# Gate and up products of a feed-forward phase in one 512-column and one 256-column matmul instead of three of 256 columns

## What is computed

```python
def swiglu(h, w_gate, w_up, w_down):
    return (jax.nn.silu(h @ w_gate) * (h @ w_up)) @ w_down
# x = x + 0.5 * swiglu(rmsnorm(x, g), ...)   D_MODEL 1024, D_FF 2816, 256 tokens
```

## Time and profile before

| | us |
|---|---|
| median of 3 runs | 2785.74 (2781.83 to 2786.46) |
| the profiled execution | 2786.89 |
| its span in the trace | 2785.1 |

### The profile page before, as it was taken

The page is one execution under the profiler, slowest core; times in us unless marked ns, Lnnn a source line. Parts: engine busy times, 40 slices in busy tenths (PEclk is TensorE's granted clock), DMA queues, the critical chain, the costliest instruction groups (busy, mean ns, idle before and its releaser), DMA issues.

```text
span 2785.1 us, 40580 instructions
## 1 busy us (share of the span) xinstructions
PE 2703.0 (97%) x17436; PEld 2435.1 (87%) x17436; DVE 1724.8 (62%) x2119; ACT 1381.9 (50%) x1758; POOL 283.4 (10%) x294
## 2 busy tenths in 40 slices
PE   9999999999998999999998998999999989999999
PEld 8997779999987789999997877899999978878998
DVE  5567765555557665555567777565555686776654
ACT  5455545344445644444466645443444575454443
POOL 0004010000004010000012124100000021232000
PEclk9999999999999999999999999999999999999999
DMA  7555445555554345555555343555555553434553
GB/s 241 194 171 166 136 152 181 182 179 189 191 180 134 130 160 189 189 182 182 183 161 163 112 133 110 173 181 185 181 182 188 172 163 107 147 111 152 182 186 132
DMA packets 335760, 461.65 MB, mean 166 GB/s; under 512 B 18010, under 2 KB 254556, under 8 KB 335580
## 3 DMA queue, kind: packets, MB, share of 16 engines
q1 hardware_dynamic: 335580, 459.05, 50.1%
HBM read 457.97 MB, written 1.05 MB: 165 GB/s over the span
## 4 chain that ended last, share of the span: by engine, by line
PE 86%; DVE 6%; ACT 5%; POOL 1%; issue 1%; DMA 0%; SPq 0%; ACTq 0%; DVEq 0%; POOLq 0%
PE PS L99 83%; DVE WL L108 2%; PE PS L102 2%; ACT WH L105 2%; DVE SB L113 1%; POOL T L108 1%; DVE XB L116 1%; ACT SB L105 0%; ACT JK L105 0%; DMA ST<-in_ffn_w_gate 0%; ACT L105 0%; DVE ME L108 0%; DVE SB L119 0%; DVE RL L116 0%; ACT XH L105 0%
## 5 line engine op out<-in xcount | busy, mean ns | idle before, releaser
L108 DVE TENSOR_TENSOR WL<-ST,WH 128x2048 fp32r<-128x2048 f32 (+3 forms) x442 | 1012.6, 2292 | 529.4 <-ACT WH L105 529.0
L105 ACT ACTIVATE WH<-ST 128x2048 fp32r<-128x2048 f32 (+3 forms) x442 | 831.1, 1881 | 771.3 <-PE PS L99 762.1
L99 PE MATMUL PS<-XH,WH 128*128 128x256 f32 x3456 | 986.0, 285 | 1.4 <-DVE XL L116 1.1
L99 PE MATMUL PS<-XL,WH 128*128 128x256 f32 x3456 | 981.6, 284 | 0.0
L99 PE MATMUL PS<-XH,WL 128*128 128x256 f32 x3456 | 981.5, 284 | 0.0
L99 PEld LDWEIGHTS PS<-XH,WH 128*128 128x128 f32 x3456 | 666.8, 193 | 6.9 <-DVE XL L116 1.7
L99 PEld LDWEIGHTS PS<-XL,WH 128*128 128x128 f32 x3456 | 667.1, 193 | 2.8
L99 PEld LDWEIGHTS PS<-XH,WL 128*128 128x128 f32 x3456 | 666.8, 193 | 0.0
L99 PE MATMUL PS<-WH,RH 128*128 128x512 f32 (+1 forms) x1056 | 412.8, 391 | 2.7 <-ACT KV L105 1.5
L99 PE MATMUL PS<-WL,RH 128*128 128x512 f32 (+1 forms) x1056 | 410.2, 388 | 0.0
L99 PE MATMUL PS<-WH,RL 128*128 128x512 f32 (+1 forms) x1056 | 409.2, 387 | 0.0
(11 more groups left out here) (243 smaller groups left out, 1996.7 us busy)
## 6 DMA issues: line engine op xcount, KB each, us to landing
ST<-in_ffn_w SPq DMA_DIRECT2D x132, 1024.0 KB, 5.0
ST<-in_w_in SPq DMA_DIRECT2D x106, 1024.0 KB, 5.1
ST<-in_ffn_w_down SPq DMA_DIRECT2D x44, 1024.0 KB, 4.8
ST<-in_ffn_w_gate SPq DMA_DIRECT2D x43, 1024.0 KB, 5.1
ST<-in_ffn_w_up SPq DMA_DIRECT2D x43, 1024.0 KB, 5.1
ST<-in_w_ssd_out SPq DMA_DIRECT2D x16, 1024.0 KB, 4.9
ST<-in_w_branch SPq DMA_DIRECT2D x8, 1024.0 KB, 4.8
ST<-in_w_out SPq DMA_DIRECT2D x8, 1024.0 KB, 5.0
```

The lines of the kernel that those rows point to most:

```text
L99: return self.eng.matmul(o, l, r, start=start, stop=stop) if self.eng else Said()
L105: return self.eng.activation(o, v, f, **kw) if self.eng else Said()
L108: return self.eng.tensor_tensor(o, a, b, op) if self.eng else Said()
```

## The change

The two parts of X now lie side by side for each k (`XHL`, [128, 8, 2, 256]), and XH and XL are views of it. A g or u tile takes, for each k and f, one matmul of 512 columns (weights WH, moving XH and XL of this k) into a whole bank, and one of 256 columns (weights WL, moving XH) into columns 0:256 of it. So a bank holds two sums, which are added when it is emptied: ScalarE copies columns 256:512 of two banks to SBUF (GB for a gate, UB for an up), and VectorE adds columns 0:256 from PSUM to it (into GS, US). The multiply by RBC and the product with the Silu read SBUF alone. Every gate now takes banks 4 and 5, every up banks 6 and 7, and they are free when that add is done (`gs`, `us`). Nothing else is changed: the mixers use XH and XL through the views.

```diff
--- before.py
+++ after.py
@@ -30,6 +30,7 @@
     FFN += [("g", _i), ("u", _i), ("d", _i - 2)]
 FFN += [("d", NP - 2), ("d", NP - 1)]
 UP_AT = {i: FFN.index(("u", i)) for i in range(NP)}
+GATE_AT = {i: FFN.index(("g", i)) for i in range(NP)}
 MIX2 = [("xbc", 0), ("xbc", 1), ("xbc", 2), ("uq", 0), ("uq", 1), ("uq", 2), ("ukv", 0), ("ukv", 1), ("uq", 3),
         ("xbc", 3), ("gate2", 0), ("xbc", 4), ("xbc", 5), ("gate2", 1), ("xbc", 6), ("xbc", 7), ("xbc", 8),
         ("xbc", 9), ("mla", 0), ("xbc", 10), ("xbc", 11), ("mla", 1), ("z", 0), ("z", 1), ("z", 2), ("gate1", 0),
@@ -346,8 +347,8 @@
     ST = sb("ST", [128, NS, 2048], F32)
     WH = sb("WH", [128, NR, 2048], F32R)
     WL = sb("WL", [128, NR, 2048], F32R)
-    XH = sb("XH", [128, 8, T], F32R)
-    XL = sb("XL", [128, 8, T], F32R)
+    XHL = sb("XHL", [128, 8, 2, T], F32R)
+    XH, XL = XHL[:, :, 0, :], XHL[:, :, 1, :]
     X = sb("X", [128, 2, DM], F32)
     R2 = where[0]
     RH = sb("RH", [128, 16, T], F32R)
@@ -385,6 +386,7 @@
     ANG = [ar("ANG0", [128, 3, 2, 8], 28736), ar("ANG1", [128, 3, 2, 32], 28992)]
 
     GS, US = ar("GS", [128, 2, 2, T], 2048), ar("US", [128, 2, 2, T], 2048 + 4096)
+    GB, UB = ar("GB", [128, 2, T], 32768), ar("UB", [128, 2, T], 32768 + 2048)
     HB = RH[:, :, :].rearrange("p (a b) t -> p a b t", b=2)
     HL = RL[:, :, :].rearrange("p (a b) t -> p a b t", b=2)
 
@@ -677,9 +679,8 @@
                 if last:
                     e.also("tile", tile)
                 continue
-            which, b = what == "u", 4 + 2 * (i % 2)
-            if not which:
-                clear(b, b + 1)
+            b = 4 + 2 * (what == "u")
+            clear(b, b + 1)
             for k in range(8):
                 if s == 0 and k == 3:
                     turn_x(e, p, "", 1)
@@ -688,13 +689,10 @@
                 if s == 0:
                     e.wait_ge(*at("xl", p, "", k))
                 for f in range(2):
-                    o, fs = PS[:, b + f, which * 256:which * 256 + 256], of(f)
-                    e.matmul(o, wh[:, k, fs], XH[:, k, :], k == 0, False)
-                    e.matmul(o, wh[:, k, fs], XL[:, k, :], False, False)
-                    m = e.matmul(o, wl[:, k, fs], XH[:, k, :], False, k == 7)
+                    e.matmul(PS[:, b + f, :], wh[:, k, of(f)], XHL[:, k, :, :].rearrange("p a t -> p (a t)"), k == 0, False)
+                    m = e.matmul(PS[:, b + f, 0:256], wl[:, k, of(f)], XH[:, k, :], False, k == 7)
             m.then_inc(*e.done("tile", tile))
-            if which:
-                freed[b] = freed[b + 1] = ("m", p, i)
+            freed[b] = freed[b + 1] = ("us" if what == "u" else "gs", p, i)
             if s == 2:
                 r_row(e, p, 3)
 
@@ -1190,6 +1188,16 @@
             if p == 0 and s == 24:
                 scalar_tables(e)
             for i in range(NP):
+                if s == UP_AT[i] + 1:
+                    e.wait_ge(*at("tile", t0 + UP_AT[i]))
+                    if i:
+                        e.wait_ge(*at("us", p, i - 1))
+                    e.activation(UB[:, :, :], PS[:, 6:8, 256:512], ACT.Copy).then_inc(*e.done("ub", p, i))
+                if s == GATE_AT[i] + 1:
+                    e.wait_ge(*at("tile", t0 + GATE_AT[i]))
+                    if i:
+                        e.wait_ge(*at("gs", p, i - 1))
+                    e.activation(GB[:, :, :], PS[:, 4:6, 256:512], ACT.Copy).then_inc(*e.done("gb", p, i))
                 if s == max(UP_AT[i] + 1, 3):
                     e.wait_ge(*at("gg", p, i))
                     e.activation(GS[:, i % 2], GS[:, i % 2], ACT.Silu).then_inc(*e.done("silu", p, i))
@@ -1608,10 +1616,8 @@
                                     ALU.subtract).then_inc(*e.done("hl", p, i))
             for i in range(NP):
                 if s == max(UP_AT[i] + 1, 3):
-                    b = 4 + 2 * (i % 2)
-                    e.wait_ge(*at("tile", t0 + UP_AT[i]))
                     e.wait_ge(*e.last())
-                    e.tensor_tensor(GS[:, i % 2], PS[:, b:b + 2, 0:256], RBC[:, :].unsqueeze(1).to_broadcast([128, 2, T]),
+                    e.tensor_tensor(GS[:, i % 2], GS[:, i % 2], RBC[:, :].unsqueeze(1).to_broadcast([128, 2, T]),
                                     ALU.mult).then_inc(*e.done("gg", p, i))
             if s == 0:
                 split_x_lo(e, p, "", 1)
@@ -1624,11 +1630,18 @@
             if s == 2:
                 row_end(e, p, 3)
             for i in range(NP):
+                if s == UP_AT[i] + 1:
+                    e.wait_ge(*at("ub", p, i))
+                    e.wait_ge(*e.last())
+                    e.tensor_tensor(US[:, i % 2], PS[:, 6:8, 0:256], UB[:, :, :], ALU.add).then_inc(*e.done("us", p, i))
+                if s == GATE_AT[i] + 1:
+                    e.wait_ge(*at("gb", p, i))
+                    e.wait_ge(*e.last())
+                    e.tensor_tensor(GS[:, i % 2], PS[:, 4:6, 0:256], GB[:, :, :], ALU.add).then_inc(*e.done("gs", p, i))
                 if s == max(UP_AT[i] + 1, 3):
-                    b = 4 + 2 * (i % 2)
                     e.wait_ge(*at("silu", p, i))
                     e.wait_ge(*e.last())
-                    e.tensor_tensor(US[:, i % 2], GS[:, i % 2], PS[:, b:b + 2, 256:512], ALU.mult).then_inc(*e.done("m", p, i))
+                    e.tensor_tensor(US[:, i % 2], GS[:, i % 2], US[:, i % 2], ALU.mult).then_inc(*e.done("m", p, i))
             if p == 0 and s == 22:
                 vector_tables(e)
             if p == 0 and s == 26:
```

## The result

| | us |
|---|---|
| before, median of 5 runs | 2785.72 (2781.21 to 2786.46) |
| changed, median of 5 runs | 2794.85 (2792.53 to 2797.38) |
| ratio, 95% interval | 1.0038 (1.0025 to 1.0052) |
| span of the profiled execution, before and changed | 2785.1 and 2795.6 |

What follows compares the result with a forecast made beforehand. TensorE's matmul pace was taken as the bound (busy 97% of the span). A gain of 36.6 and 0.3 us against 32.1 lost (16.6 + 12.6 + 2.9) made it 4.8 us faster: 2781.0 against the median, range 2774 to 2791.

Steps and rivals of the forecast that it cites:

- matmuls: Gate and up tiles: a 512 and a 256 replace three 256-column matmuls, 0.347 us instead of 0.360; 36.6 us gained.
- idle spot in phase 0: Feed-forward phase 0: an idle spot of TensorE goes away, 0.3 us gained.
- wait of gate 1: First tiles of each phase: gate 1 waits for VectorE's add of gate 0; 16.6 us lost, 7.1 in phase 0.
- wait of up 1: First tiles: up 1 waits for up 0's add, which stands behind RBC's copy; 1.57 x 8 phases, 12.6 us lost.
- clock in phase 0: Phase 0: the stop of 7 us at gate 1 should halve TensorE's clock; 2.9 us lost.
- waits at short stops, clock: First tiles: stops of 1.6 us leave TensorE's clock alone; costed at nothing.
- emptying in the steady state: Later tiles: the added ScalarE copies and VectorE adds are covered by slack; costs nothing.
- The rival with 0.355: Gate and up tiles: the fixed part stays or half goes, pair 0.355 us; gain 14 us, total 2803; chance 0.08.
- The clock's rivals: Gate 1 and up 1: 13 waits of about 1.6 us halve the clock; 21 us, total 2802; chance 0.08.
- The prediction's bound: Clock at short stops: a stretch with 2.03 us idle fell to 0.73; at most 1.6 us lost per stop.
- Steady state: Rival, later tiles: each group of three waits for an emptied bank; 18 us more, total 2799; chance 0.04.
- waits aren't there: Rival, first tiles: the waits at gate 1 and up 1 don't occur; total 2749; chance 0.05.

Runs made afterwards that it cites:

- the three-matmul kernel: Changed kernel with the widening undone (three 256-column matmuls) and the copy-and-add emptying kept; 2812.27 us, ratio 1.0097 to the kernel before.
- the kernel with 512 columns throughout: Changed kernel with the low weights' matmul also 512 columns wide, all else kept; 3061.23 us in a single run.
- the two reorders: Changed kernel with RBC's copy moved behind the add of up 0: 2782.81 us; or with the first gate emptied early: 2781.57 us.
- two and two: Changed kernel with, per k, the two 512-column matmuls first, then the two 256-column ones; 2780.1 us, ratio 0.9982 to the kernel before.

## Why the prediction was wrong

2781.0 with a range to 2791.0 was forecast, and 2794.85 came: outside, and of the other sign. Point by point:

| step | predicted | measured |
|---|---|---|
| matmuls | -36.6 | -19.0 (64 x 0.186, and 7.1 in the first tiles) |
| idle spot in phase 0 | -0.3 | gone |
| wait of gate 1 | 16.6 | 15.4 (6.3 + 8.2 + 0.8) |
| wait of up 1 | 12.6 | 12.5 (8 x 1.56); 12.0 by undoing it |
| clock in phase 0 | 2.9 | 2.1 (28.51 to 32.7 us at half) |
| waits at short stops, clock | 0 | 0 |
| emptying in the steady state | 0 | 0 (16.980 us a group in the three-matmul kernel) |
| sum | -4.8 | 10.7 by these rows (-0.3 for the idle spot); 10.5 by the spans, 10.6 by the ratio, 9.1 by the medians |

- **The failed step** is "I take 0.347, since each border's excess is made good at the other." In the steady state it isn't. A pair there costs 0.3528 us, near the upper bound of 0.355 that the same paragraph gave, and the excess runs on into the down tile. Only in some of the first tiles did the forecast price come true (0.3466, phase 0), and nothing in the prediction told the two apart. The trace of before had a sign of it: the early starts of a 512-column run lie 0.233 and 0.236 apart where later ones lie 0.2264, and that excess lasts for five matmuls and sums to some 28 ns, against 6 ns won back at the other border (0.11 instead of 0.12). I read two borders as each other's mirror when they weren't, and drew the range for the pair, 0.345 to 0.349, far narrower than the bounds. The rival with 0.355 had 0.08 and came closest, its price of the pair being nearly right. The mechanisms it named are out: the wider stream by the kernel with 512 columns throughout, and the weight load by the stretches at 0.3466, which have the same loads beside the same matmuls.
- **The waits** were right in place and cause, and near in size: with the clock's part 30.0 us against 32.1. In the three-matmul kernel they cost 26.5 us by the trace; gate 1 is 1.36 us late there in five phases and not 1.65, since the tiles ahead of it are longer. Undone one at a time they give 12.0 and 13.3 us by the medians, and both together 23.9 (26.2 in the traces' first tiles), with a wait of 2.5 us left at phase 0's up 1.
- **The clock's rivals** fell as the profile of before had it: stops of 1.6 us leave it at 1.00. The Trainium skill ("TensorE: Matmul & The Clock Gate", "A second HAM failure mode: psum-queue depth-cycling") warns of short idle spots between groups of matmuls; here none of the thirteen lowered the clock. The prediction's bound, that 2.03 us idle once did, has its like in the stop of 2.5 us that did in one kernel and did not in two.
- **Steady state and "waits aren't there"**: both out, by the three-matmul kernel and by the list of waits.
- The rows, the spans and the ratio agree on 10.5 to 10.7 us; the median of five is 9.1, inside the interval of the ratio, 7.0 to 14.5 us.
- **The range** had its own slip: the low end of 2774 is 7 us below 2781, while its three parts add up to 10.5 (5.6 + 2.9 + 2), so 2770.5; the high end of 2789 is their plain sum. It changed nothing, as the result lies above it.

The Trainium skill ("TensorE: Matmul & The Clock Gate", Back-to-back issue gap) gives N/2.4 plus about 2.5 ns for an isolated warm matmul, which the prediction held against a stream. The streams of these kernels, a weight load with each matmul, don't follow it: 512 columns start 0.2267 us apart, 13 ns over the columns.

## What to carry to other kernels

Price a new alternation of instructions by the alternation, or by both bounds, never by the means of the pure runs; try matmuls of one width in runs of two or more, which was worth 13 to 16 us here. Read a pace at several places: one stretch at the forecast pace doesn't vouch for the next. When PSUM banks get fewer turns, look at the first tiles of each stage, where emptying stands behind work that was never urgent: each of the two reorders was worth 11 to 15 us here, the whole edit to the matmuls 19. And free the second wait in the same step, since the first one hides it.

## What the hardware showed that I had not expected

Matmuls of 512 and 256 columns in turn ran at two paces in one kernel: 0.3528 us a pair in all tiles behind a phase's first down tile, and 0.3466 in some of the first tiles, which is what whole runs of each width take (0.347). The slow pace came only where the width changes: 512 and 384 in turn took 0.4063 where N/2.4 plus 13 ns each gives 0.400, and 512 and 512 took 0.4533, as that sum says. With two and two it was 0.348, so it isn't a fixed price per change. What puts a stretch at one pace or the other was not found.
